# First token tile's second search stage inside the query blocks, and the next layer's first modulation tiles inside attention, in a two-layer diffusion backbone

## What is computed

```python
mod = jax.nn.silu(c) @ w_mod[l] + b_mod[l]      # 6 x 1024 numbers: shift, scale, gate, twice
h = rms_norm(x, norm_g[l, 0]) * (1 + scale1) + shift1
...                                             # q, k, v, attention in three head groups, w_out
h2 = rms_norm(x, norm_g[l, 1]) * (1 + scale2) + shift2
# peer_ffn(h2, ...)
q = (x @ wq).reshape(n, PEER_HEADS, 2, PEER_DQ // 2)
s = jnp.einsum('nhcd,hckd->nhck', q, keys).astype(jnp.float32)
s1, i1 = lax.top_k(s[:, :, 0], PEER_TOPK)       # first search stage: 16 of 128, twice a head
s2, i2 = lax.top_k(s[:, :, 1], PEER_TOPK)
cand = (s1[..., :, None] + s2[..., None, :]).reshape(n, PEER_HEADS, PEER_TOPK * PEER_TOPK)
sc, ci = lax.top_k(cand, PEER_TOPK)             # second search stage: 16 of 256
e = (jnp.take_along_axis(i1, ci // PEER_TOPK, axis=-1) * N_KEYS
     + jnp.take_along_axis(i2, ci % PEER_TOPK, axis=-1))     # expert numbers
g = jax.nn.softmax(sc, axis=-1)
a = jax.nn.gelu(jnp.einsum('tkd,td->tk', u[eb], xb))
y = jnp.einsum('tk,tkd->td', (a * gb.astype(a.dtype)), v[eb])
```

## Time and profile before

| | before |
|---|---|
| median of 3 runs | 5012.46 us (5008.81 to 5022.82) |
| profiled execution | 4980.59 us, its span 4978.8 us |
| PE busy | 3670.4 us (74%) |
| DVE busy | 2815.9 us (57%) |
| ACT busy | 1427.4 us (29%) |
| POOL busy | 1387.5 us (28%) |
| DMA | 1460.22 MB, mean 293 GB/s |

### The profile page before, as it was taken

One profiled execution on the slowest core, in us unless ns is written; L12 is line 12 of the kernel. 1 busy time (PEld: TensorE's weight loads), 2 busy tenths in 40 slices (PEclk: granted clock), 3 DMA queues, 4 the chain that ended last, 5 costly groups with the idle time before them and its releaser, 6 DMA issues.

```text
span 4978.8 us, 42425 instructions
## 1 busy us (share of the span) xinstructions
PE 3670.4 (74%) x14116; PEld 1690.3 (34%) x14116; DVE 2815.9 (57%) x6028; ACT 1427.4 (29%) x4223; POOL 1387.5 (28%) x1475
## 2 busy tenths in 40 slices
PE   5777588677777777777768776857777777777776
PEld 2453445232222222332236344532222222322222
DVE  3543365665766756654454434567657567575544
ACT  2233322223222232232221433222222322322222
POOL 1011100333343433333310110013434333334332
PEclk7897789899999999999989868989999999999999
DMA  4122023999999999999921211129999999999997
GB/s 173 48 80 75 9 63 107 386 413 416 420 421 419 419 422 413 413 409 412 421 89 54 85 51 31 60 122 415 416 422 419 419 420 416 420 407 410 422 420 294
DMA packets 213532, 1460.22 MB, mean 293 GB/s; under 512 B 23936, under 2 KB 24192, under 8 KB 48448
## 3 DMA queue, kind: packets, MB, share of 16 engines
q0 software_dynamic: 185952, 1355.11, 65.7%
q1 hardware_dynamic: 27360, 102.39, 6.3%
HBM read 1453.21 MB, written 4.19 MB: 293 GB/s over the span
## 4 chain that ended last, share of the span: by engine, by line
PE 39%; DMA 36%; DVE 12%; ACT 8%; issue 4%; POOL 0%; SPq 0%; ACTq 0%; DVEq 0%; POOLq 0%
DMA work<-expert_dram,work 26%; PE psum L716 17%; PE psum L502 10%; DMA hT<-expert_dram,work 10%; DVE work L1304 4%; ACT work L842 3%; PE psum L616 2%; PE psum L596 2%; PE psum L633 2%; ACT work L920 2%; PE psum L568 2%; DVE hT L1304 1%; DVE work L1042 1%; ACT work L910 1%; PE psum L538 1%
## 5 line engine op out<-in xcount | busy, mean ns | idle before, releaser
L716 PE MATMUL psum<-work 128*128 128x512 f32 x3416 | 1612.3, 616 | 555.5 <-ACT work L920 550.4
L1304 DVE SCALAR_TENSOR_TENSOR work<-work,psum 128x1024 f32<-128x1024 f32 x854 | 1041.5, 1220 | 826.9 <-DMA work<-expert_dram,work 824.9
L1361 POOL DMA_INDIRECT work<-expert_dram,work x854 | 827.2, 969 | 1487.7 <-PE psum L716 1316.1
L716 PEld LDWEIGHTS psum<-work 128*128 128x128 f32 x3416 | 627.6, 193 | 1530.2 <-ACT work L920 881.3
L716 PE MATMUL psum<-hT,work 128*128 128x512 f32 x1704 | 795.4, 610 | 306.5 <-ACT work L920 302.7
L910 ACT ACTIVATE work<-work,xinv 128x2 f32<-128x2 f32 x640 | 189.1, 295 | 2338.3 <-DVE work L1304 1554.7
L1304 DVE SCALAR_TENSOR_TENSOR hT<-hT,psum 128x1024 f32<-128x1024 f32 x426 | 519.7, 1220 | 414.4 <-DMA hT<-expert_dram,work 414.2
L1361 POOL DMA_INDIRECT hT<-expert_dram,work x426 | 418.0, 981 | 805.0 <-PE psum L716 634.6
L716 PEld LDWEIGHTS psum<-hT,work 128*128 128x128 f32 x1704 | 309.7, 191 | 786.1 <-ACT work L920 467.8
L502 PE MATMUL psum<-hT,split 128*128 128x128 f16 (+1 forms) x2880 | 432.5, 311 | 52.5 <-DVE hT L1077 52.5
L920 ACT ACTIVATE work<-const,work 128x128 f32<-128x128 f32 x1280 | 434.1, 386 | 0.0
(11 more groups left out here) (152 smaller groups left out, 2737.7 us busy)
## 6 DMA issues: line engine op xcount, KB each, us to landing
ring<-w_mod_dram SPq DMA_DIRECT2D x96, 512.0 KB, 3.6
ring<-w_in_dram SPq DMA_DIRECT2D x40, 512.0 KB, 3.6
ring<-w_query_dram SPq DMA_DIRECT2D x32, 512.0 KB, 3.5
work<-expert_dram,work POOLq DMA_INDIRECT x854, 8.4
ring<-w_out_dram SPq DMA_DIRECT2D x16, 512.0 KB, 3.5
hT<-expert_dram,work POOLq DMA_INDIRECT x426
work<-rpb_dram POOLq DMA_DIRECT2D x2, 2688.0 KB, 14.6
xT<-xT_dram SPq DMA_DIRECT2D x1, 2560.0 KB, 10.7
```

The lines of the kernel that those rows point to most:

```text
L716: last = pe.matmul(out[:, cols_], diag[:, n % NDIAG, :], rows[n % NBUF][:, D + 512 * half:D + 512 * half + 512], start=(s == 0), stop=(s = ...
L1304: dve.scalar_tensor_tensor(u, u, 1.0, pair[t % 2], ALU.mult, ALU.mult, accum_out=act_in[:, s:s + 1]).then_inc(dot_done, 1)
L1361: pool.indirect_dma_start(rows[n % NBUF], None, a[f"expert{l}"], bass.IndirectOffsetOnAxis(expert[:, t % 2, s:s + 1], 0)).then_inc(row_in[ ...
```

## The change

- **Second search stage head by head.** `first_head(h)` is new: for one head it adds the candidates (256 columns), finds the 16 largest, takes the numbers apart, and makes the head's 16 expert numbers. VectorE runs it inside the query blocks: head 0 in iteration s = 3 behind `first_keys(1)`, head 1 at s = 5, and so on, head 7 at s = 17. The last one sets `expert_ready`. `choose` is left for tiles 1 to 4.
- **Weights apart.** `first_weights` does for tile 0 what is left of the softmax: it runs at the start of `experts`, behind `expert_ready`.
- **Modulation.** `late_mods(l)` lists tiles 16 to 47 of layer l and, for layer 0, tiles 0 to 15 of layer 1 behind them: 48 in attention of layer 0, steps k = 2 to 49. Their loads move ahead of `wout` in the ring, their turns and `modulation(1, ...)` to the end of attention of layer 0. PSUM columns and SBUF places for their sums change accordingly. Layer 1's attention keeps 32.

```diff
+def late_mods(l):
+
+    return [(l, j) for j in range(FIRST_MOD, NMOD)] + [(l + 1, j) for j in range(FIRST_MOD) if l + 1 < L]
...
         plan += [("mod", l, j) for j in range(FIRST_MOD, NMOD)]
+        if l + 1 < L:
+            plan += [("mod", l + 1, j) for j in range(FIRST_MOD)]
         plan += [("wout", l, i) for i in range(KC)]
         plan += [("wq", l, i) for i in range(HC)]
-        if l + 1 < L:
-            plan += [("mod", l + 1, j) for j in range(FIRST_MOD)]
...
             if c < FIRST_CHUNK:
-                return 3, (0, y_at - 512)[l], modps[l]
+                return (3, 0, modps[0]) if l == 0 else (7, next_at + 512 * c, modps[1])
...
-                    j = FIRST_MOD + k - MOD_PAIR
-                    if FIRST_MOD <= j < NMOD:
-                        mod_tile(l, j)
+                    if 0 <= k - MOD_PAIR < len(late_mods(l)):
+                        mod_tile(*late_mods(l)[k - MOD_PAIR])
...
-                for c in range(FIRST_CHUNK, NCHUNK):
-                    mod_turn(l, c)
+                for m, j in late_mods(l)[::KC]:
+                    mod_turn(m, j // KC)
...
             def experts(l):
-                if l + 1 < L:
-                    mod_chunks(l + 1, 0, FIRST_CHUNK)
-                    mod_turn(l + 1, FIRST_CHUNK - 1)
                 pe.wait_ge(scores_in, HC * (l + 1))
                 turn_rows(l, 0)
                 for t in range(TT):
                     out = pair[2 + t % 2]
-                    if t == 1 and l + 1 < L:
-                        pe.wait_ge(mod_read, 3)
...
-                    if 0 <= j < MOD_LATE and j % KC == KC - 1:
-                        mod_copy(l, FIRST_CHUNK + j // KC)
+                    if 0 <= j < len(late_mods(l)) and j % KC == KC - 1:
+                        mod_copy(late_mods(l)[j][0], late_mods(l)[j][1] // KC)
...
                 modulation(l, FIRST_MOD, NMOD, 2 * l + 2)
+                if l + 1 < L:
+                    modulation(l + 1, 0, FIRST_MOD, 3)
...
                         first_keys(s - 2)
+                        if s % 2:
+                            first_head((s - 3) // 2)
...
+            def first_head(h):
+
+                eight = slice(TOPK * h, TOPK * h + 8), slice(TOPK * h + 8, TOPK * h + 16)
+                slots = slice(TOPK * h, TOPK * h + TOPK)
+                c, spare = (buf[:, 2 * P * h:2 * P * h + 2 * P] for buf in (cand, alt))
+                dve.tensor_copy(topf[:, h], topi[:, 2 * TOPK * h:2 * TOPK * h + 2 * TOPK].rearrange(
+                    "p (c k) -> p c k", k=TOPK))
+                link(dve.tensor_tensor(c.rearrange("p (a b) -> p a b", a=TOPK),
+                                       top[:, h, 0, :].unsqueeze(2).to_broadcast([P, TOPK, TOPK]),
+                                       top[:, h, 1, :].unsqueeze(1).to_broadcast([P, TOPK, TOPK]), ALU.add))
+                link(dve.max(sel[:, eight[0]], c))
+                dve.max_index(seli[:, eight[0]], sel[:, eight[0]], c)
+                link(dve.match_replace(spare, sel[:, eight[0]], c, LOWEST))
+                link(dve.max(sel[:, eight[1]], spare))
+                link(dve.max_index(seli[:, eight[1]], sel[:, eight[1]], spare))
+                link(dve.tensor_scalar(hi[:, slots], seli[:, slots], 4, None, ALU.logical_shift_right))
+                link(dve.tensor_scalar(seli[:, slots], seli[:, slots], 15, None, ALU.bitwise_and))
+                dve.tensor_copy(route[:, 0, slots], hi[:, slots])
+                link(dve.tensor_copy(route[:, 1, slots], seli[:, slots]))
+                eq = work[:, alt_at:alt_at + 2 * HC * P].rearrange("p (c h s a) -> p c h s a", c=2, h=HEADS, a=TOPK)[:, :, h]
+                link(dve.tensor_tensor(eq, route[:, :, slots].unsqueeze(3).to_broadcast([P, 2, TOPK, TOPK]),
+                                       iota4, ALU.is_equal))
+                link(dve.tensor_tensor(eq, eq, topf[:, h].unsqueeze(2).to_broadcast([P, 2, TOPK, TOPK]), ALU.mult))
+                link(dve.tensor_reduce(route[:, :, slots], eq, AX_X, ALU.add))
+                last = dve.scalar_tensor_tensor(expert[:, 0, slots], route[:, 0, slots], float(NK), route[:, 1, slots],
+                                                ALU.mult, ALU.add)
+                if h == HEADS - 1:
+                    last.then_inc(expert_ready, 1)
...
+            def first_weights(l):
+
+                s2 = sel.rearrange("p (h k) -> p h k", h=HEADS)
+                link(dve.tensor_copy(gsum[:, 0:HEADS], s2[:, :, 0]))
+                dve.tensor_tensor(s2, s2, gsum[:, 0:HEADS].unsqueeze(2).to_broadcast([P, HEADS, TOPK]),
+                                  ALU.subtract).then_inc(sub_ready, 1)
+                slot_weights(l, 0)
...
-                choose(l, 0, lambda: None, lambda: 0)
+                first_weights(l)
...
-                    if t == 0 and l + 1 < L:
-                        modulation(l + 1, 0, FIRST_MOD, 3)
```

41 lines of the change are left out of this document (19 added, 22 removed).

## The result

| | before | after |
|---|---|---|
| median (lowest to highest) | 5008.81 us (5003.5 to 5022.82), 5 runs | 4931.22 us (4915.23 to 4933.93), 5 runs |
| ratio after to before | | 0.9835, 95% interval 0.9813 to 0.9858 |
| profiled execution | 4980.59 us | 4933.93 us |

What follows compares the result with a forecast made beforehand. Nearly two thirds of the time was put in the two expert stages, with DMA engines always busy. The terms, 53.6 - 3.8 - 3.0 + 5.5 = 52.3 us, taken from 5012.5 gave 4960 us, range 4942 to 4984.

Steps and rivals of the forecast that it cites:

- Hand-over: Last key scores to first gather: first gather at 846.2 instead of 873.04, 26.8 us gained a layer, together 53.6.
- Head: VectorE's search and expert numbers for one head, 15 instructions: 5.8 us, bounds 5.0 and 7.5.
- Stalls: Query blocks: TensorE's block_sum waits 0.5 us for VectorE's reduction in four blocks a layer, 3.8 us lost in all.
- The rule that was weighed here: VectorE instruction count: if VectorE's time counted on the path, the gain would become a loss of 28 us over both layers.
- Attention's costs: Attention of layer 0: tiles sticking out 0.7, mod_copy 0.9, more transposes 0.9, one more modulation 0.5; 3.0 us lost.
- Clock: C pairs (third part of attention), layer 0: tiles filling TensorE's gaps raise its granted clock; 5.5 us won, middle of 11.
- Base and expert stages: Whole kernel: expert stages keep their length; difference between profiled 4980.6 and median 5012.46 us taken over.
- All of it: Rival, C pairs of layer 0: all of the 11 us of clock is given back, time 4954 us; chance 17%.
- heads longer than 5.8: Rival, VectorE: heads of say 7.5 us, 14 us more stalls and 3 at the ends, 4977; chance 8%.
- exposed tiles: Rival, C pairs of layer 0: tiles not hidden since ScalarE waits too, 30 us, 4996 at most; chance 4%.
- a gather held by something else: Rival, first gather: weights or turned rows hold it, so it comes no earlier, 5010 us; chance 3%.
- a slower kernel: Rival, query blocks: VectorE becomes the bound; slower from heads of about 10.5 us, about 5028 at 12; chance 3%.

Runs made afterwards that it cites:

- the second run of the changed kernel: The changed kernel, unchanged, timed again: median 4925.93 us, ratio 0.9829 to the kernel before.

## Why the prediction was off

- **Hand-over: right.** 26.8 a layer forecast, 26.85 and 26.83 measured; first gather 7.98 behind the last scores, 8.0 by the sum (1.71 + 5.7 + 0.58).
- **Head: right.** 5.8 forecast, 5.88 measured, largely out of rows for other widths: 512-column passes took 0.69 each where 0.68 was read.
- **Stalls: near.** 0.5 us in four blocks a layer, together 3.8 forecast. Four blocks a layer stall, and each costs 0.60, together 4.8; TensorE takes 0.38 of it as waiting, the rest I read as its start behind a wait. The query blocks are longer by 3.4 and 2.4, together 5.8: layer 0's further 1.1 us (0.2 in the second run of the changed kernel) are the late return of the clock in the first block, which the kernel with the tiles alone shows as well. VectorE works 23.6 us more in the whole (2839.5 against 2815.9), and besides the last head only these stalls reach the path. The rule that was weighed here, the Trainium skill's "Minimize op *count*, not sems" (VectorE: DVE Perf Modes, Rules for kernel authors), would have made it a loss; it holds for VectorE's own time, and these stages are not bound by that.
- **Attention's costs: near.** 3.0 forecast; pair 49 to the end takes 21.58 instead of 19.48, 2.1, and nothing sticks out in the C pairs (84.16, with an idle matmul for the tile 84.12). The w_out loads and the 16 tile loads cost nothing: the stretch at 89 GB/s is as long as the one at 1.
- **Clock: the step that failed.** The prediction read the low level's share rightly off the grant: 62% of 116 us, "2.9 of 9.75" each, which is 21.6 us to be had. Then it cut twice: the C pairs would reach only the 0.85 of the pairs that carry tiles, 11 us, and of that "I take the middle, **5.5 won**". The first cut took a row of other pairs, the second had none; and the full 11 that the prediction ascribes to staying at the higher clock is only what a grant of 0.85 gives, staying there is the 21.6. The pairs that carry tiles are no measure for the others: with a tile and one idle matmul they stay at 0.85, while the C pairs show 1.00 with a single idle matmul and with a tile alike. Measured is 107.80 to 84.16, **23.6 us**; with the costs behind pair 49 and 3.3 more in the pairs ahead, which vary by themselves, attention of layer 0 is 18.2 shorter (21.4 in the second run), where the forecast had 2.5. That is 16 of the 25.3 us by which the prediction missed, and 19 of the 35.0 in the second run. Layer 1's attention, 323.14 for 326.59, shows the same step of 3.4 us as the kernel before shows against itself (323.16 in two of its six), so I count it as no effect of the change.
- **Base and expert stages: the range.** The forecast took the difference over from a profiled execution to the median. By stages the changed kernel is some 66 us shorter outside the expert stages (4978.8 - 3248.6 = 1730.2 before, 1728.4 and 1726.0 in its other profiled executions; 1659.8 and 1663.5 after), the medians differ by 77.6 and 87.3. The 11 to 21 us between are open, and without them the time would have been inside the range. What the runs show is that the spread goes with the clock: 85 executions of the kernel before were timed with their mean granted clock; the six below 4990 us have 0.933 in the mean, the eighteen above 5020 have 0.923. All three profiled executions of before (4980.59, 4983.34, 4994.14) lie below the medians, at 0.930 to 0.932; the two of after have 0.938 and 0.939. So I take the longer expert stages after (3272.3 and 3260.9 against 3248.6, 3253.1, 3266.2) for part of the spread rather than an effect, but no profile of before in a typical execution was caught, and it is not shown.
- **Rivals.** "All of it" was the nearest case, at 4954, and itself short by half; heads longer than 5.8, exposed tiles, a gather held by something else and a slower kernel did not come about.

By the prediction's own terms with the measured sizes: 53.7 - 5.8 + 18.2 = 66 us, and 53.7 - 4.9 + 21.4 = 70 in the second run of the changed kernel: 4942 to 4946 from the base of 5012.5, at the lower end of the range. The rest, down to the measured 4931.22, is the open part.

## What to carry to other kernels

Where a stretch of regular small gaps is granted less than the full clock, price the whole low share of it, and probe it with idle matmuls in each gap before arguing about how much of it will come back; look in the trace whether the probe adds time to the engine, runs beside what is there, or sticks out of the gap at the lower clock. When a chain of work ahead of a transfer phase is cut, look at what else was using that time: here 8 MB of weight loads did, and the heads alone lost some 22 us to them in the first 64 gathers, out of 53.7 won. Here a piece of VectorE's inside TensorE's period cost its excess over the slack, and from there on 1.37 us of piece cost 1.37 in nearly every stall; cut pieces so that nothing of them stands ahead of the last result that the next stage waits for.
